# A hybrid encoder trunk: mixer halved by token parity and spread over its input projection, and the keys' mean by a block matrix with a re-ordered end of the attention

## Chip, cores and metric

One core of one Trainium2 chip. The metric is device microseconds of one execution; the kernel before has a median of 1862.9 us over 3 runs (1862.3 to 1864.59).

## What is computed

Two sequences of 256 tokens pass two layers with the same weights, model width 1024. Each layer is half an FFN, a mixer, half an FFN. The mixer of layer 0 pools four channel groups over windows of 2, 4, 8 and 16 tokens beside a long convolution by FFT; the mixer of layer 1 is a neighbourhood attention of 16 heads of 64 with normalised queries and keys. Cut to these two:

```python
def pool_hyena_mixer(xn, ...):
    p = xn @ w_in                                  # 1024 -> 512 + 3 * 512
    a = pool_mixer(p[..., :POOL_WIDTH], pool_w, pool_scale)   # (win_sum / cnt - u) @ w_grp * scale
    hb = short_conv(p[..., POOL_WIDTH:], short_w, short_b)    # three taps
    x0, x1, v = hb[..., :512], hb[..., 512:1024], hb[..., 1024:]
    k_f = hyena_filter_fft(L, ...)                 # rfft of (MLP of t * decays), 2 L points
    yh = fftconv(v * x1, k_f, h_bias) * x0         # irfft(rfft(u, 2 L) * k_f)[:L] + u * bias
    return concatenate([a, yh]) @ w_out

def na_mixer(xn, w_qkv, gq, gk, rpb, w_o):
    q, k, v = split(xn @ w_qkv)
    q, k = rmsnorm(q, gq), rmsnorm(k, gk)          # mean of squares over the 64 features of a head
    out = softmax(where(col_mask, q @ k.T * scale + bias, -inf)) @ v
    return out @ w_o
```

## The kernel before

All 512 tokens lie as columns and the features on partitions, 8 chunks of 128 for the width. The program runs through phases one after the other: the first FFN, w_in, w_out, two FFNs, qkv, w_o, the last FFN. Each engine has a block of its own (sync, scalar, vector, tensor, gpsimd) whose instructions are written out in the order in which it runs them; semaphores join the engines, so the order by hand decides everything. A **unit** of a projection is 128 output features by 512 tokens in one PSUM bank: 8 steps of k, each three fp32r matmuls (`three`, L1241: high by high, low by high, high by low parts, L1242, L1245, L1246). Its weights arrive by DMA, ACT rounds them to the high part (`split_high`, L480) and VectorE subtracts that for the low part (`split_low`, L489), about two units ahead. A unit can have **hooks**: other work of TensorE put in front of step k. Matmuls outside the units are plain fp32 and show as two records each.

w_in has 16 units, (i, j) for i in 0 to 3 and j in 0 to 3. For each i VectorE takes the banks out times the norm factor (`scaled`, L883), ACT and VectorE make the three-tap convolutions (L548, L901, L904), VectorE the product v * x1, TensorE turns that product (L1367), and POOL makes the window sums (L1633 to L1644). The filter's decays (ACT, L794, L797) and its products and sums (L1196 to L1207) lie in between. Only after all 16 units come the Fourier steps, as matmuls with cosine and sine matrices: filter spectra (L1541, 8 matmuls), token spectra (L1553, 16), pool matmuls (L1560, 4), inverse (L1569, 32); VectorE multiplies spectra (L1224) and POOL sums them. Then w_out starts.

qkv runs 8 pairs of heads of three units (query, key, value); the attention of pair p - 1 is worked in hooks of pair p (`attention`, L1370 on TensorE, L1084 on VectorE, L679 on ACT). At a pair's end the means of squares of queries and keys are made by two-column matmuls (`squares_mean`, L1415), ACT takes the square root (L730), VectorE the reciprocal of 128x16 (L1139), copies the keys' part wide (L1141), TensorE turns it (`key_factor`, L1423), VectorE scales the key (L1145) and takes the value (L883, tile vt). From the third pair on, the first unit of a pair is in the bank of the value unit before it, and `bank_read` makes it wait until vt has been taken. `three` and the wait in `unit`:

```python
if ph.name == "qkv":
    return (0, 1, 2 if isinstance(i, int) and i == 0 else 0)[j]
...
if ks[0] == 0 and (ph.name == "qkv" or isinstance(i, int) and i == 0 and j == 0):
    pe.wait_ge(*bank_read(ph, i, j))
```

After pair 7, w_o's first two units (7 of their 8 steps) hold the last pair's scores, turns (L1393) and values (L1402) in hooks; the rest of w_o follows.

## Time and profile before

| what | value |
|---|---|
| median of 3 runs | 1862.9 us (1862.3 to 1864.59) |
| the profiled execution's own time | 1859.85 us |
| its span, first to last instruction | 1858.1 us |
| TensorE busy | 1848.1 us, 99% |
| VectorE busy | 1310.8 us, 71% |
| ACT busy | 819.9 us, 44% |
| POOL busy | 292.3 us, 16% |
| granted TensorE clock | 1.00 |
| share of the chain that ended last | TensorE 98%, VectorE 1% |

The profile is of one execution. Busy times are sums over the span; the chain is followed back from the last instruction, so a share of 98% says that TensorE's own instructions, one behind the other, fill the time. Time starts in each row are us from the start of the span.

### The profile page before, as it was taken

How to read it: one execution, taken by the hardware profiler on the slowest of the kernel's cores; microseconds unless marked ns; L12 is line 12 of the kernel's file. 1: busy time of each engine (PE TensorE's matmuls, PEld its weight loads, DVE VectorE, ACT ScalarE, POOL GpSimd, SP SyncE). 2: the span in 40 equal slices, each digit the busy share in tenths (PEclk: the TensorE clock that was granted, in tenths of full speed). 3: DMA queues.
4: the chain of work that ended last, by engine and by line, in shares of the span. 5: the costliest groups of instructions: out<-in, count | busy, mean ns of one | idle time of the engine just before them, and what ended most of it. 6: DMA issues, size and time to landing. Idle time of an engine off the chain costs nothing.

```text
span 1858.1 us, 26529 instructions
## 1 busy us (share of the span) xinstructions
PE 1848.1 (99%) x10116; PEld 1581.6 (85%) x10116; DVE 1310.8 (71%) x2086; ACT 819.9 (44%) x1344; POOL 292.3 (16%) x247
## 2 busy tenths in 40 slices
PE   9999999999999999999999999999999999999999
PEld 7898988977688988989889898898777788989889
DVE  7686865975466867768767686686776666868666
ACT  5343443643244433435534343465655543433333
POOL 0210401203301203102021130111111002104011
PEclk9999999999999999999999999999999999999999
DMA  5244236632032222348323223662222232332356
GB/s 186 75 142 119 91 114 173 166 127 91 23 114 102 102 97 86 114 123 229 102 74 131 91 91 114 181 156 86 70 80 79 74 114 74 113 110 90 111 159 162
DMA packets 79737, 210.70 MB, mean 113 GB/s; under 512 B 15144, under 2 KB 28105, under 8 KB 79626
## 3 DMA queue, kind: packets, MB, share of 16 engines
q1 hardware_dynamic: 56800, 182.48, 28.6%
q0 software_dynamic: 9216, 16.78, 5.3%
q10 hardware_dynamic: 13610, 9.93, 1.9%
q8 instruction: 73, 1.20, 0.3%
q14 instruction: 38, 0.31, 0.1%
HBM read 190.29 MB, written 3.93 MB: 105 GB/s over the span
## 4 chain that ended last, share of the span: by engine, by line
PE 98%; DVE 1%; ACT 0%; DMA 0%; issue 0%; SPq 0%; ACTq 0%; DVEq 0%
PE bank L1290 25%; PE bank L1292 25%; PE bank L1291 25%; PE bank L1242 6%; PE bank L1245 5%; PE bank L1246 5%; PE bank L1402 1%; PE bank L1569 1%; PE bank L1553 1%; PE bank L1415 1%; PE bank L1393 1%; PE bank L1423 0%; PE bank L1541 0%; PE bank L1382 0%; DMA x<-in_x_tokens 0%; PE bank L1345 0%
## 5 line engine op out<-in xcount | busy, mean ns | idle before, releaser
L1290 PE MATMUL bank<-xh,whr 128*128 128x512 f32 x1408 | 551.5, 392 | 2.3 <-DVE wlr L466 1.0
L1291 PE MATMUL bank<-xl,whr 128*128 128x512 f32 x1408 | 549.1, 390 | 0.0
L1292 PE MATMUL bank<-xh,wlr 128*128 128x512 f32 x1408 | 549.0, 390 | 0.0
L457 ACT ACTIVATE whr<-rest 128x512 fp32r<-128x512 f32 (+1 forms) x445 | 273.2, 616 | 455.4 <-PE bank L1292 445.5
L466 DVE TENSOR_TENSOR wlr<-rest,whr 128x512 fp32r<-128x512 f32 (+1 forms) x445 | 323.3, 730 | 124.5 <-ACT whr L457 121.7
L1290 PE MATMUL bank<-hsh,whr 128*128 128x256 f32 x1232 | 349.1, 283 | 0.4 <-issue 0.3
L1291 PE MATMUL bank<-hsl,whr 128*128 128x256 f32 x1232 | 348.6, 283 | 0.0
L1292 PE MATMUL bank<-hsh,wlr 128*128 128x256 f32 x1232 | 348.6, 283 | 0.0
L1290 PEld LDWEIGHTS bank<-xh,whr 128*128 128x128 f32 x1408 | 265.1, 188 | 60.0 <-issue 2.1
L1292 PEld LDWEIGHTS bank<-xh,wlr 128*128 128x128 f32 x1408 | 265.0, 188 | 55.7
L1291 PEld LDWEIGHTS bank<-xl,whr 128*128 128x128 f32 x1408 | 265.1, 188 | 55.4 <-issue 1.0
L457 ACT ACTIVATE whr<-raw_area 128x512 fp32r<-128x512 f32 (+1 forms) x243 | 147.6, 608 | 238.7 <-PE bank L1292 233.8
L1290 PEld LDWEIGHTS bank<-hsh,whr 128*128 128x128 f32 x1232 | 236.3, 192 | 1.4 <-DVE wlr L466 0.5
L1291 PEld LDWEIGHTS bank<-hsl,whr 128*128 128x128 f32 x1232 | 236.4, 192 | 0.5
L1292 PEld LDWEIGHTS bank<-hsh,wlr 128*128 128x128 f32 x1232 | 236.4, 192 | 0.0
L466 DVE TENSOR_TENSOR wlr<-raw_area,whr 128x512 fp32r<-128x512 f32 (+1 forms) x243 | 173.1, 715 | 61.8 <-ACT whr L457 60.4
L976 DVE SCALAR_TENSOR_TENSOR x<-bank,x 128x256 f32<-128x256 f32 (+1 forms) x288 | 146.3, 508 | 5.3 <-PE bank L1292 3.7
L928 DVE TENSOR_TENSOR ga<-bank,rbc 128x512 f32<-128x512 f32 x88 | 60.8, 691 | 77.6 <-PE bank L1292 77.5
L1242 PE MATMUL bank<-xh,whr 128*128 128x512 f32 x256 | 103.5, 404 | 0.0
L1588 POOL TENSOR_TENSOR raw_area<-raw_area 128x384 f32<-128x384 f32 (+1 forms) x14 | 17.3, 1235 | 527.1 <-DMA raw_area<-in_ffn_w_down 527.1
L1245 PE MATMUL bank<-xl,whr 128*128 128x512 f32 x256 | 100.0, 391 | 0.0
L1246 PE MATMUL bank<-xh,wlr 128*128 128x512 f32 x256 | 99.8, 390 | 0.0
(188 smaller groups left out, 2114.6 us busy)
## 6 DMA issues: line engine op xcount, KB each, us to landing
rest<-in_ffn_w_up SPq DMA_DIRECT2D x62, 512.0 KB, 4.7
rest<-in_ffn_w_gate SPq DMA_DIRECT2D x61, 512.0 KB, 3.8
rest<-in_ffn_w_down SPq DMA_DIRECT2D x54, 512.0 KB, 4.6
raw_area<-in_ffn_w_gate SPq DMA_DIRECT2D x26, 512.0 KB, 3.7
raw_area<-in_ffn_w_up SPq DMA_DIRECT2D x26, 512.0 KB, 4.7
raw_area<-in_ffn_w_down SPq DMA_DIRECT2D x26, 512.0 KB, 4.6
raw_area<-in_w_qkv SPq DMA_DIRECT2D x24, 512.0 KB, 3.4
rest<-rest POOLq DMA_DIRECT2D x38, 256.0 KB, 4.6
```

Source lines behind the costliest of these rows:

```text
L457: act.activation(whr[:, at:at + st.kb, :].rearrange("p k c -> p (k c)"), weights(st, buf)[:, 0, :], ACT.Copy).then_inc(high, 1)
L466: dve.tensor_tensor(wlr[:, at:at + st.kb, :].rearrange("p k c -> p (k c)"), weights(st, buf)[:, 0, :], whr[:, at:at + st.kb, :].bitcast(F3 ...
L928: dve.tensor_tensor(ga[st.tiles % 2][:, :], bank[st.bank][:, :], rbc[:, :], ALU.mult).then_inc(evac, 1)
L976: dve.scalar_tensor_tensor(out=out, in0=src, scalar=0.5 * sign, in1=out, op0=ALU.mult, op1=ALU.add)\
L1242: pe.matmul(out, wh[w][:, k, :], hi[:, at, :], start=start, stop=False)
L1245: pe.matmul(out, wh[w][:, k, :], lo[:, at, :], start=False, stop=False)
L1246: return pe.matmul(out, wl[w][:, k, :], hi[:, at, :], start=False, stop=stop)
L1290: pe.matmul(out, whr[:, at, :], hi, start=start, stop=False, skip_group_check=onto)
L1291: pe.matmul(out, whr[:, at, :], lo, start=False, stop=False, skip_group_check=onto)
L1292: return pe.matmul(out, wlr[:, at, :], hi, start=False, stop=stop, skip_group_check=onto)
L1393: last = pe.transpose(bank[2 if h % 2 else 6][:, k * SEQ + t * P:k * SEQ + (t + 1) * P], sc[:, h, t, k * P:(k + 1) * P], ident)
L1402: last = pe.matmul(bank[7][a_ * HD:(a_ + 1) * HD, s * SEQ:(s + 1) * SEQ], vs[:, 2 * s + k, a_ * HD:(a_ + 1) * HD], pt[:, h % 2, k, :], sta ...
```

## The change

Three edits are made at once.

- **The mixer.** Tokens are parted into even and odd ones, so that the cosine and sine matrices have 128 frequencies by 128 tokens of a parity: half as many or half as wide matmuls (filter spectra 4 of 512 columns, L1562; token spectra 16 of 256, L1586; inverse 32 of 128, L1599). Sums and differences of the halves give the full spectra; VectorE makes them and the products, and POOL only the window sums. The work is done for each i by itself, and TensorE's part stands in hooks of w_in's units and of w_out's first two, whose steps go in the order 3, 2, 1, 4, 5, 0, 6, 7. Units of one i are now v, x1, pool, x0; the largest pool window comes first. ACT's and VectorE's orders for w_in are written anew.
- **The keys.** Their mean of squares is one plain 128x512 matmul with a block matrix of 1/64 (`key_mean`), so that it stands for each key on all partitions of its head. ACT's square root and VectorE's reciprocal run over 128x512 (L808, L1367), and the key is scaled from SBUF (L1369). The wide copy and `key_factor` are gone. The queries keep their two-column matmuls (`query_mean`).
- **The end of the attention.** w_o's third unit is begun early in bank 3 and shares the last pair's hooks with the first two; its split comes first on ACT and VectorE, and the banks of the first two units are taken after the fourth unit's split.

```diff
-                return w_in[bass.ds((3 - j) * KH + i, 1)]
+                return w_in[bass.ds((3 * KH + i, 2 * KH + i, KH - 1 - i, KH + i)[j], 1)]
...
+                if attends and not projects:
+                    split_high(act, by["w_o"], 0, 2)
...
-                    act.wait_ge(ms_mm, p + 1)
-                    act.activation(rqk[:, :, :, :], bank[3][:, 0:4 * TT].rearrange("p (a t h) -> p a t h", a=2, t=TT),
-                                   ACT.Sqrt, bias=cst[:, C_EPS:C_EPS + 1]).then_inc(ms_std, 1)
+                    act.wait_ge(k_mean, p + 1)
+                    act.activation(rk[:, :], bank[3][:, :], ACT.Sqrt, bias=cst[:, C_EPS:C_EPS + 1]).then_inc(k_std, 1)
                     if attends:
                         act.wait_ge(s_mm, 4 * p)
                     act.activation(qh[:, :], qt[:, :], ACT.Copy).then_inc(qh_done, 1)
+                    act.wait_ge(q_mean, p + 1)
+                    act.activation(rq[:, :, :], bank[3][:, 0:2 * TT].rearrange("p (t h) -> p t h", t=TT), ACT.Sqrt,
+                                   bias=cst[:, C_EPS:C_EPS + 1]).then_inc(q_std, 1)
...
+                def products(i):
+                    dve.wait_ge(wide_done, 2 * (i + 1))
+                    dve.wait_ge(kf_done, 2)
+                    if i:
+                        dve.wait_ge(spec_done, 2 * i)
+                    for n, out in enumerate((t1, t2)):
+                        dve.tensor_tensor(out[:, :, :, :], wide[:, :, :, :],
+                                          kfb[:, :, n, i * P:(i + 1) * P].unsqueeze(2).to_broadcast([P, 2, 2 * NSEQ, P]),
+                                          ALU.mult).then_inc(prod_done, 1)
+                def product_sums(i):
+                    dve.wait_ge(prod_done, 2 * (i + 1))
+                    for n, op in enumerate((ALU.subtract, ALU.add)):
+                        own_, other = slice(NSEQ * n, NSEQ * (n + 1)), slice(NSEQ * (1 - n), NSEQ * (2 - n))
+                        dve.tensor_tensor(t1[:, :, own_, :], t1[:, :, own_, :], t2[:, :, other, :], op).then_inc(sum_done, 1)
...
+                split(0, 0)
+                norm_factor(NORM_OF["w_in"])
+                split(0, 1)
+                take(0, 0)
+                take(0, 1)
+                sums_cleared(NORM_OF["w_in"])
+                taps(0, 0)
+                taps(0, 1)
+                product(0)
+                split(0, 2)
+                to_pool(0)
+                filter_in_time()
+                split(0, 3)
+                take(0, 3)
+                filter_sums()
+                taps(0, 3)
+                for i in range(1, KH):
+                    if i > 1:
+                        gate_with(i - 2)
+                    split(i, 0)
+                    take(i, 0)
+                    if i > 1:
+                        products(i - 1)
+                    taps(i, 0)
+                    if i == 1:
+                        filter_in_frequency()
+                    take(i, 1)
+                    split(i, 1)
+                    taps(i, 1)
+                    product(i)
+                    if i == 1:
+                        frequencies(0)
+                    else:
+                        product_sums(i - 1)
+                        conv_low(i - 2)
+                    split(i, 2)
+                    to_pool(i)
+                    if i == 1:
+                        products(0)
+                        pool_low(0)
+                        product_sums(0)
+                        spectra(0)
+                    else:
+                        spectra(i - 1)
+                        pool_low(i - 1)
+                    if i == KH - 1:
+                        frequencies(i)
+                        products(i)
+                    split(i, 3)
+                    take(i, 3)
+                    if i < KH - 1:
+                        taps(i, 3)
+                        frequencies(i)
+                i = KH - 1
+                product_sums(i)
+                spectra(i)
+                gate_with(i - 1)
+                taps(i, 3)
+                pool_low(i)
+                conv_low(i - 1)
+                gate_with(i)
+                conv_low(i)
...
-                    dve.wait_ge(ms_std, p + 1)
-                    dve.reciprocal(rqk[:, :, :, :], rqk[:, :, :, :]).then_inc(rqk_done, 1)
-                    dve.wait_ge(rqk_done, p + 1)
-                    dve.tensor_copy(kwide[:, :, :].rearrange("p t (h c) -> p t h c", h=2),
-                                    rqk[:, 1, :, :].unsqueeze(3).to_broadcast([P, TT, 2, HD])).then_inc(kw_done, 1)
-                    dve.wait_ge(kb_mm, p + 1)
-
-                    dve.scalar_tensor_tensor(out=kt[:, :], in0=kt[:, :], scalar=gqk[:, 0:1], in1=bank[3][:, :],
+                    dve.wait_ge(k_std, p + 1)
+                    dve.reciprocal(rk[:, :], rk[:, :]).then_inc(rk_done, 1)
+                    dve.wait_ge(rk_done, p + 1)
+                    dve.scalar_tensor_tensor(out=kt[:, :], in0=kt[:, :], scalar=gqk[:, 0:1], in1=rk[:, :],
                                              op0=ALU.mult, op1=ALU.mult).then_inc(kn_done, 1)
+                    dve.wait_ge(q_std, p + 1)
+                    dve.reciprocal(rq[:, :, :], rq[:, :, :]).then_inc(rq_done, 1)
                     if attends:
                         dve.wait_ge(v_mm, p)
                     scaled(ph, p, 2, vt[:, :], unit_bank(ph, p, 2))
...
+                def filter_frequencies():
+                    pe.wait_ge(filt_done, 8)
+                    for n in range(4):
+                        q, cs = n // 2, n % 2
+                        pe.matmul(bank[4 + n][:, :], dft[:, cs, q, :], (hdif if cs else hsum)[:, q, :], start=True,
+                                  stop=True).then_inc(kf_mm, 1)
...
+                def inverse(c):
+                    pe.wait_ge(spec_done, 2 * (c + 1))
+                    pe.wait_ge(ut_done, min(c + 2, KH))
+                    if c:
+                        pe.wait_ge(gated, c)
+                    for s in range(NSEQ):
+                        for q in range(2):
+                            at = (2 * s + q) * P
+                            for cs in range(2):
+                                last = pe.matmul(bank[6][:, at:at + P], spec[c % 2][:, q, NSEQ * cs + s, :],
+                                                 idft[:, q, cs, :], start=cs == 0, stop=cs == 1)
+                    last.then_inc(inv_mm, 1)
...
+                norm = NORM_OF["w_in"]
+                unit(ph, 0, 0, waits=[(xl_done, chunk_base(norm) + k + 1) for k in range(KD)])
+                unit(ph, 0, 1, hooks={1: lambda: norm_mean(norm)})
+                unit(ph, 0, 2, hooks={4: filters})
+                unit(ph, 0, 3)
+                for i in range(1, KH):
+                    if i == 1:
+                        unit(ph, 1, 0)
+                        unit(ph, 1, 1, hooks={4: filter_frequencies})
+                        unit(ph, 1, 2, hooks={2: lambda: turn_u(0), 5: lambda: frequencies(0), 6: lambda: pool_mm(0)})
+                    else:
+                        unit(ph, i, 0, hooks={4: lambda: inverse(i - 2)})
+                        unit(ph, i, 1, hooks={5: lambda: pool_mm(i - 1)})
+                        unit(ph, i, 2)
+                    last = {7: lambda: inverse(KH - 2)} if i == KH - 1 else {}
+                    unit(ph, i, 3, hooks={1: lambda: turn_u(i), 4 + (i < KH - 1): lambda: frequencies(i), **last})
+                ph = by["w_out"]
+                order = [3, 2, 1, 4, 5, 0, 6, 7]
+                parts = [(pool_al, KH - k) if k < KH else (conv_al, k - KH + 1) for k in range(KD)]
+                unit(ph, 0, 0, waits=parts, ks=order[:5], order=order, hooks={2: lambda: pool_mm(KH - 1)})
+                unit(ph, 0, 1, ks=order[:5], order=order, hooks={1: lambda: inverse(KH - 1)})
+                for j in range(2):
+                    unit(ph, 0, j, waits=parts, ks=order[5:], order=order)
...
-                def squares_mean():
-                    pe.wait_ge(sqq_done, p + 1)
+                def key_mean():
                     pe.wait_ge(sqk_done, p + 1)
+                    pe.wait_ge(heads_done, 4)
                     if attends:
                         pe.wait_ge(vs_done, p)
-                    for a_, sq in enumerate((sqq, sqk)):
-                        for t in range(TT):
-                            at = a_ * 2 * TT + 2 * t
-                            last = pe.matmul(bank[3][:, at:at + 2], sq[:, t * P:(t + 1) * P], cst[:, C_HEAD:C_HEAD + 2],
-                                             start=True, stop=True)
-                    last.then_inc(ms_mm, 1)
-
-                def key_factor(pair=p):
-
-                    pe.wait_ge(kw_done, pair + 1)
+                    pe.matmul(bank[3][:, :], heads[:, :], sqk[:, :], start=True, stop=True).then_inc(k_mean, 1)
...
                 def turn_values():
                     pe.wait_ge(evac, by["qkv"].group(p - 1, 2) + 1 + EVAC_CREDIT)
-                    pe.wait_ge(kn_done, p)
+                    pe.wait_ge(q_std, p)
                     for t in range(TT):
...
-                    unit(ph, 0, 0, waits=parts, ks=ks, hooks={1: leftovers, 2: first_scores, 6: lambda: scores(1)})
+                    unit(ph, 0, 0, waits=parts, ks=ks, hooks={1: leftovers, 2: first_scores})
                     pe.wait_ge(evac, ph.group0 - 1 + EVAC_CREDIT)
-                    unit(ph, 0, 1, ks=ks, hooks={0: lambda: (turn(0), turn(1)), 3: first_values,
-                                                 4: lambda: (turn(2), turn(3)), 5: lambda: second_values(p - 1)})
+                    unit(ph, 0, 1, ks=ks, hooks={1: lambda: scores(1), 4: lambda: (turn(0), turn(1))})
+                    pe.wait_ge(vs_done, PAIRS)
+                    unit(ph, 0, 2, ks=range(6), hooks={0: first_values, 2: lambda: (turn(2), turn(3)),
+                                                               4: lambda: second_values(p - 1)})
                     for j in range(2):
                         unit(ph, 0, j, waits=parts, ks=[KD - 1])
+                    unit(ph, 0, 2, waits=parts, ks=range(6, KD))
...
-                if isinstance(p, int):
-                    unit(ph, p, 0, hooks={1: lambda: key_factor(0), 4: leftovers})
-                else:
-                    unit(ph, p, 0, hooks={2: leftovers})
+                unit(ph, p, 0, hooks={2: leftovers})
                 first_scores()
                 unit(ph, p, 1)
-                unit(ph, p, 2, hooks={1: second_scores, 4: first_values, 5: squares_mean, 7: key_factor})
+                unit(ph, p, 2, hooks={1: second_scores, 4: first_values, 5: key_mean, 7: query_mean})
```

VectorE at the end of a pair, before (rsum: softmax sums, rqk: both root means, kt and vt: key and value, ms_std: ACT's root, kb_mm: the turned factor):

```order
L1107 TENSOR_SCALAR sc<-sc,rsum 128x256 [waits rs_done]
L1107 TENSOR_SCALAR sc<-sc,rsum 128x256
L1139 RECIPROCAL rqk<-rqk 128x16 [waits ms_std]
L1141 COPY kwide<-rqk 128x512 [waits rqk_done]
L1145 SCALAR_TENSOR_TENSOR kt<-kt,small,bank 128x512 [waits kb_mm]
L879 REGISTER_ALU [waits v_mm]
L883 TENSOR_TENSOR vt<-bank,rbc 128x512 [waits unit_done]
```

and with the change (rk, rq: root means of keys and queries apart):

```order
L1330 TENSOR_SCALAR sc<-sc,rsum 128x256 [waits rs_done]
L1330 TENSOR_SCALAR sc<-sc,rsum 128x256
L1367 RECIPROCAL rk<-rk 128x512 [waits k_std]
L1369 SCALAR_TENSOR_TENSOR kt<-kt,small,rk 128x512 [waits rk_done]
L1372 RECIPROCAL rq<-rq 128x8 [waits q_std]
L947 REGISTER_ALU [waits v_mm]
L951 TENSOR_TENSOR vt<-bank,rbc 128x512 [waits unit_done]
```

The reciprocal has grown from 128x16 to 128x512 and stands ahead of kt and vt; the copy and the wait for kb_mm are gone.

VectorE behind w_in's last units, before (spec, ga, ua: parts of the products of spectra, kf: filter spectra):

```order
L489 TENSOR_TENSOR wlr<-raw_area,whr 128x1024 [waits high]
L883 TENSOR_TENSOR ppad<-bank,rbc 128x2x256 [waits unit_done]
L489 TENSOR_TENSOR wlr<-raw_area,whr 128x1024 [waits high]
L1224 TENSOR_TENSOR spec<-bank,kf 128x512 [waits u_mm,tap_done,kf_done]
L1224 TENSOR_TENSOR spec<-bank,kf 128x512
L1224 TENSOR_TENSOR ga<-bank,kf 128x512 [waits u_mm]
L1224 TENSOR_TENSOR ua<-bank,kf 128x512
```

and with the change, around unit (1,2) (wide: a spectrum's halves joined, kfb: filter spectra, t: products, ppad: the pool input that POOL waits for):

```order
L501 TENSOR_TENSOR wlr<-raw_area,whr 128x1024 [waits high]
L951 TENSOR_TENSOR ppad<-bank,rbc 128x2x256 [waits unit_done]
L1041 TENSOR_TENSOR t<-wide,kfb 128x1024 [waits kf_done,wide_done]
L1041 TENSOR_TENSOR t<-wide,kfb 128x1024
L1075 SCALAR_TENSOR_TENSOR al<-bank,small,ah 128x512 [waits pool_ah]
L1050 TENSOR_TENSOR t<-t 128x2x256 [waits prod_done]
L1050 TENSOR_TENSOR t<-t 128x2x256
L1058 TENSOR_TENSOR spec<-t 128x512 [waits sum_done]
L1058 TENSOR_TENSOR spec<-t 128x512
L501 TENSOR_TENSOR wlr<-raw_area,whr 128x1024 [waits high]
```

The products now stand between the splits of two units, right behind ppad, and what TensorE's first inverse needs is the spec at the end.

TensorE in unit (2,0) with the change, where no Fourier step stood before:

```order
L1428 MATMUL bank<-xh,whr 128x512
L1431 MATMUL bank<-xl,whr 128x512
L1432 MATMUL bank<-xh,wlr 128x512
L1599 MATMUL bank<-idft,spec 128x128 [waits ut_done,spec_done]
L1599 MATMUL bank<-idft,spec 128x128 x7
L1428 MATMUL bank<-xh,whr 128x512
```

The inverse's eight matmuls stand ahead of step 4 and wait for spec; the unit's own steps are behind them.

## Rows read from the trace of the kernel before

**Rows 1.** The page's fourth part: the chain that ended last, shares of the span by engine.
```profile
PE 98%; DVE 1%; ACT 0%; DMA 0%; issue 0%; SPq 0%; ACTq 0%; DVEq 0%
```

**Rows 2.** The chain in order of time (start, duration, engine and line), w_in to w_out.
```profile
365.76 0.45 PE bank L1242
...
460.17 6.87 PE bank L1541 x16
467.04 13.73 PE bank L1553 x32
...
484.20 13.81 PE bank L1569 x64
```

**Rows 3.** TensorE in order of time in w_out (start, duration, line, operation, out<-in, count).
```profile
499.24 0.39 PE L1242 MATMUL bank<-ah,whr 128*128 128x512 f32 x1
...
540.04 0.39 PE L1242 MATMUL bank<-ah,whr 128*128 128x512 f32 x1
```

**Rows 4.** VectorE in order of time, the norm ahead of w_in and w_in.
```profile
374.61 3.35 DVE L870 RECIPROCAL rbc<-rbc 128x512 f32<-128x512 f32 x1 [0.70 <-ACT rbc L537]
...
395.35 2.48 DVE L1196 SCALAR_TENSOR_TENSOR filt<-decay,bank 128x512 f32<-128x512 f32 x4 [1.65 <-ACT decay L797]
...
398.51 1.23 DVE L1202 TENSOR_TENSOR hsum<-filt 128x1024 f32<-128x1024 f32 x1
...
401.52 1.21 DVE L489 TENSOR_TENSOR wlr<-raw_area,whr 128x1024 fp32r<-128x1024 f32 x1
...
461.78 2.16 DVE L489 TENSOR_TENSOR wlr<-raw_area,whr 128x1024 fp32r<-128x1024 f32 x1 [1.32 <-ACT whr L480]
```

**Rows 5.** POOL in order of time, window sums of w_in.
```profile
393.86 1.08 POOL L1633 TENSOR_TENSOR win<-ppad 128x542 f32<-128x542 f32 x1 [26.12 <-DVE ppad L883]
395.02 1.30 POOL L1640 TENSOR_TENSOR win<-win,icnt 128x512 f32<-128x512 f32 x1
...
461.77 4.45 POOL L1633 TENSOR_TENSOR win<-win 128x538 f32<-128x538 f32 x3
```

**Rows 6.** ACT in order of time, the norm ahead of w_in and the decays.
```profile
373.89 0.69 ACT L537 ACTIVATE rbc<-bank,small 128x512 f32<-128x512 f32 x1
...
394.09 2.19 ACT L797 ACTIVATE decay<-absd,small 128x1024 f32<-128x1024 f32 x2
```

**Rows 7.** Busy time by windows: PE, PEld, DVE, ACT, POOL, clock, DMA share, GB/s.
```profile
378.00:380.00 2.00, 2.00 (x10) 1.65 (x10) 0.97 (x1) 0.93 (x1) 0.00 (x0) 1.00 0.15 61
```

**Rows 8.** TensorE in order of time, the end of a pair of the attention.
```profile
1389.23 0.95 PE L1415 MATMUL bank<-small,sqq 128*128 128x2 f32 x8
...
1394.94 0.50 PE L1242 MATMUL bank<-xh,whr 128*128 128x512 f32 x1
```

**Rows 9.** VectorE in order of time, the same end.
```profile
1388.45 1.94 DVE L1107 TENSOR_SCALAR sc<-sc,rsum 128x256 f32<-128x256 f32 x2
...
1390.50 0.62 DVE L1107 TENSOR_SCALAR sc<-sc,rsum 128x256 f32<-128x256 f32 x2
...
1393.51 0.75 DVE L1145 SCALAR_TENSOR_TENSOR kt<-kt,small,bank 128x512 f32<-128x512 f32 x1 [1.38 <-PE bank L1423]
1394.20 0.69 DVE L883 TENSOR_TENSOR vt<-bank,rbc 128x512 f32<-128x512 f32 x1
```

**Rows 10.** ACT and POOL in order of time, the same end.
```profile
1389.49 1.28 ACT L730 ACT_TABLE_LOAD   x1
...
1388.43 1.55 POOL L1658 TENSOR_TENSOR bmask<-braw,small 128x768 f32<-128x768 f32 x1 [18.38 <-DVE nmax L1098]
1391.98 1.28 POOL L1665 TENSOR_TENSOR ql<-qt,qh 128x512 fp32r<-128x512 f32 x1 [2.00 <-ACT qh L734]
```

**Rows 11.** TensorE in order of time, the end of the attention.
```profile
1447.57 0.47 PE L1242 MATMUL bank<-oh,whr 128*128 128x512 f32 x1
...
1462.26 1.47 PE L1402 MATMUL bank<-pt,vs 128*64 128x256 f32 x8 [1.97 <-ACT pt L707]
...
1481.09 0.39 PE L1242 MATMUL bank<-oh,whr 128*128 128x512 f32 x1
```

More of the change, by code:

```diff
@@ L334, in unit_bank @@
                 return (0, 1, 2 if isinstance(i, int) and i == 0 else 0)[j]
+            if ph.name == "w_o" and isinstance(i, int) and i == 0:
+                return (0, 1, 3, 2)[j]
             return j
@@ new lines, in to_pool, with filter_in_time @@
+                def to_pool(i):
+                    scaled(ph, i, 2, ppad[:, KH - 1 - i, :, PAD:PAD + SEQ], 2, "p (s t) -> p s t")
+                def filter_in_time():
+                    for t in range(2):
+                        for half in range(2):
+                            n = 2 * t + half
+                            dve.wait_ge(filt_mm, n + 1)
+                            dve.wait_ge(dec_done, 2 + t)
+                            dve.scalar_tensor_tensor(out=filt[:, t, half, :], in0=decay[:, t, half, :], scalar=0.05,
+                                                     in1=bank[4 + n][:, :], op0=ALU.add, op1=ALU.mult)\
+                               .then_inc(filt_done, 1)
@@ L1258, in bank_read, with unit @@
                 else:
-                    look = 1 if at_start else 3
+                    look = 1 if at_start else 2 if ph.name == "w_o" and j == 2 else 3
                 return evac, ph.group(i, j) - look + EVAC_CREDIT
-            def unit(ph, i, j, waits=None, hooks={}, ks=None):
+            def unit(ph, i, j, waits=None, hooks={}, ks=None, order=None):
                 w = split_place(ph, i, j)[0]
@@ L1280, in unit @@
                         pe.wait_ge(*waits[k])
-                    last = three(bank[b][:, :], w, k, b, hi, lo, k, start=k == 0, stop=k == ph.kt - 1,
-                                 between=after if k == ph.kt - 1 else None)
-                if ks[-1] == ph.kt - 1:
+                    last = three(bank[b][:, :], w, k, b, hi, lo, k, start=k == order[0], stop=k == order[-1],
+                                 between=after if k == order[-1] else None)
+                if ks[-1] == order[-1]:
                     last.then_inc(unit_done, 1)
@@ L1496, in _ @@
                     continue
-                def first(ph=ph, name=name):
-                    if name in NORM_OF:
-                        norm = NORM_OF[name]
-                        unit(ph, 0, 0, waits=[(xl_done, chunk_base(norm) + k + 1) for k in range(KD)])
-                        unit(ph, 0, 1, hooks={1: lambda: norm_mean(norm)})
-                        rest = range(2, ph.per)
-                    else:
-                        if name == "w_o":
-                            attention(PAIRS, False, True, False)
-                            rest = range(2, ph.per)
-                        else:
-                            unit(ph, 0, 0, waits=[(al_done, k + 1) for k in range(KD)])
-                            rest = range(1, ph.per)
-                    for j in rest:
-                        unit(ph, 0, j)
-                    if name == "w_in":
-                        turn_u(0)
-                        pe.wait_ge(mix_in, 16 * 7)
-                        for n in range(4):
-                            t, half = n // 2, n % 2
-                            if n == 3:
-                                pe.wait_ge(ut_done, 1)
-                            pe.matmul(bank[4 + n][:, :], h3[:, t * P:(t + 1) * P], fwo[:, half * HW:(half + 1) * HW],
-                                      start=True, stop=True).then_inc(filt_mm, 1)
@@ L1524, in body @@
-                def body(i, last, ph=ph, name=name):
+                if name == "w_in":
+                    w_in_run(ph)
+                    continue
+                if name == "w_o":
+                    attention(PAIRS, False, True, False)
+                for j in range(3 if name == "w_o" else 2, ph.per):
+                    unit(ph, 0, j)
+                with pe.Fori(1, ph.iters) as i:
                     for j in range(ph.per):
                         unit(ph, i, j)
-                    if name == "w_in":
-                        turn_u(i)
```

454 lines of the change are left out of this document (255 added, 199 removed).

## Prediction

> **What bounds the kernel now.** I read the chain that ended last first: TensorE holds 98% of it, VectorE 1%, all else next to nothing [rows 1]. The matmuls themselves set the time; an edit pays only by taking work off TensorE, and costs only where it makes TensorE wait. Next, the chain in order of time [rows 2]: w_in begins at 365.76, and after its 16 units three stretches of plain fp32 matmuls stand alone on TensorE: filter spectra 6.87 us (L1541), token spectra 13.73 (L1553), inverse 13.81 (L1569). Then the rate of the units: from 499.24 to 540.04 [rows 3] lie 60 steps of k, three 512-column matmuls each, 0.68 a step and 5.44 a unit, without a gap. Last, the end of an attention pair [rows 8 to 10] and of the attention [rows 11], the two other places that are edited.
>
> **The mixer.** Its multiplications on TensorE [rows 2]: the filter spectra go from 8 to 4 matmuls of 512 columns, 6.87 / 2 = 3.43; the token spectra keep 16 matmuls but of 256 columns instead of 512, 13.73 / 2 = 6.87; the inverse keeps its 32 matmuls (64 records) but of 128 columns instead of 256, 13.81 / 2 = 6.9. No row has short fp32 matmuls in this number, so I take 7.1, a little over half (the two-column ones of the attention, 8 records in 0.95 [rows 8], say that a record goes down to some 0.12 at least). Turns, filter matmuls and pool matmuls stay. Sum: 3.44 + 6.86 + 6.7 = **17.0 us off TensorE**.
>
> These pieces now sit inside units, so each one whose input is late stops TensorE. I followed the new order of VectorE (quoted ahead) with durations of before: a split 1.21, a 128x1024 product or sum 1.23 [rows 4], a bank's take 0.69 [rows 9], the rest by the same rate.
> 1. filter_frequencies stands in unit (1,1) before step 4: 365.76 + five units + 0.86 + 3.43 (norm and filter matmuls) + 2.72 = about 400.0. The constants have landed by 378, from when on DMA's share is 0.15 [rows 7]; decays follow them (1.04, a table load of 1.28 and 2.19 [rows 6]), to 382.5; ACT's split(0,1) is behind them, done at 383.6. VectorE then has, in order: the split, two takes, the memset, four taps, two products, a split, to_pool, four filter products, a split, a take, memset, sum, difference and bias, 17 us with semaphore gaps: 401.5, and 402.7 if POOL's window sums hold one up. Wait: **2.0**.
> 2. inverse(0) is in unit (2,0) before step 4, 10.3 us after unit (1,2) ends (unit, turn 0.44, spectra 1.72, half a unit). VectorE's to_pool ends 2.95 after that point, then two products, pool_low, two product sums, two spectra: 5.7, done at 8.7, no wait. But the same to_pool starts POOL's five window steps, and rows show such steps and VectorE's two-input instructions taking turns: a split took 2.16 instead of 1.21 when it began beside a window sum at 461.77, and those three POOL sums took 4.45 where one alone takes 1.08 [rows 4, 5]. Taking turns, some five POOL steps of about 1.1 come between: 14.0 instead of 8.7. Wait: **3.7**.
> 3. turn_u(2) behind the same queue 1.0; inverse(3) in w_out, at the end of product sums, spectra and taps, 2.0; w_out's third split 0.4; the rest 0.6 as an allowance. Sum **4.0**.
>
> Mixer: -17.0 + 2.0 + 3.7 + 4.0 = **-7.3**. If nothing takes turns, waits 2 and parts of 3 go: about -13.6.
>
> A rule is to be weighed against rows here. In the mixer, filter products (one input in PSUM, one in SBUF) ran 2.48 for four beside POOL's 1.30 at 395.02, neither stretched [rows 4, 5], while the two-input split was. The Trainium skill ("SBUF — State Buffer", Who interferes with whom) says the same in general: a VectorE instruction with two SBUF inputs contends with a GpSimd one that reads SBUF, with the lock held for a whole instruction; one with at most one SBUF input, outside the 2-port modes, doesn't. By it the mixer's sum is as above, and the attention's long reciprocal shuts nobody out.
>
> **The keys of a pair.** Let S be the start of the mean squares, 1389.23, where now unit (p+1,0) follows at 1394.94, S + 5.71 [rows 8]. What releases it is VectorE's take of vt, 1394.20 + 0.69 [rows 9], since the unit writes the bank that vt is read from. The new chain: key_mean 0.86 (13.73 / 16), hidden by ACT's table load to S + 1.54 [rows 10]; Sqrt of 128x512, 0.69 as in the norm [rows 6], to S + 2.27; VectorE's **RECIPROCAL of 128x512, 3.35** as in the norm [rows 4], to S + 5.62, where before it took 128x16; kt 0.75 to 6.40; rq about 0.15; vt to 7.24; TensorE at S + 7.29. Removed are the copy of kwide, key_factor on TensorE and VectorE's wait for it. TensorE itself is ready earlier: means 0.86 + 0.84, three steps and turns 0.9, S + 4.65, so its work is no cover and it waits 2.6. Per pair 7.29 - 5.71 = 1.58, seven times: **+11.1**; the first pair, whose unit has another bank, waits only for vt before its turn: +0.4. ACT's kh and the next splits are 1.4 later but need to be ready only within unit (p+1,0): hidden.
>
> Bounds: if ACT's Sqrt and POOL are as above, nothing makes this smaller except a unit that isn't held by vt (rival 2); if POOL's ql (1.28, ready S + 2.9 [rows 10]) can't run beside the reciprocal, kt waits for it too (rival 3).
>
> **The end of the attention.** w_o starts at 1447.57, waits 1.97 at 1462.26 for the probabilities' copy, and unit (1,0) starts at 1481.09, 33.5 later [rows 11]. With the third unit as a filler that wait goes. But split(0,2) now stands ahead of the first maxima on VectorE (1.45 later), unit (0,3) finds its split 1.05 late since its buffer is free only after unit (0,1), and unit (1,0) finds its split behind two residuals, some 1.6 with what is left of the first wait: unit (1,0) at 32.65. **-0.85**.
>
> **Sum.** -7.3 + 11.1 + 0.4 - 0.85 = +3.35 on the profiled execution's 1859.85: 1863.2. That execution lies 3.05 under the median of 1862.9, so the forecast for the median is **1866**. About 0.2% (3.7 us) is what a measurement can tell from no change; this lies just inside.
>
> **Rivals.**
> 1. *POOL and VectorE collide less.* The window sums may begin in gaps that VectorE has for ACT's splits anyway; for it, the filter products beside POOL; against it, the stretched split. Mixer -12 to -15, so 1858 to 1862. On the fast side. Chance 0.22.
> 2. *The reciprocal doesn't gate the next unit.* If unit (p+1,0) isn't held by vt, TensorE goes on at S + 4.65, saving 1.06 a pair: 7 x 1.06 + 0.85 = 8.3 won in the attention, 15.6 in all: 1847. For it, TensorE waits nowhere for vt now in the list of waits; against it, 1394.20 + 0.69 = 1394.89 and the start at 1394.94. Chance 0.10.
> 3. *The long reciprocal shuts POOL out* (slower). Place: between rk's reciprocal and kt; price: ql's 1.28 a pair, seven times, 9.0; point: whether ql starts before or after the reciprocal ends. For it: two one-input TENSOR_SCALARs took 1.94 beside POOL's mask at 1388.43, and 0.62 without [rows 9, 10]. Against it: filter products with one input in SBUF weren't held [rows 4, 5]. 1875. By the skill's rule, the reciprocal has one SBUF input and isn't held, so this would be 0; TENSOR_SCALAR is among those that it lists with 2-port modes. Chance 0.10.
> 4. *Short matmuls aren't half as long* (slower). If 128-column inverse records took as long as 256-column ones, the saving of 6.7 goes: 1873. Against it: the chain's two-column means are down to 0.12 a record, little over half of the inverse's 13.81 / 64 = 0.216. Chance 0.08.
>
> **How the numbers follow.** The forecast has 0.50: spread of some 5 us about 1866 from stalls that I estimated (0.05 faster, 0.25 same, 0.20 slower). Rival 1 splits 0.11 faster, 0.11 same; rival 2 is faster; 3 and 4 slower. Faster 0.26, same 0.36, slower 0.38. The range goes from 1853 (rival 1 with shorter waits at the end) to 1875 (rival 3); outside are rival 2 and the far tails.
>
> **What would show it.** Mixer: TensorE's busy time between w_in's and w_out's start down by 17, its waits at L1562, L1577, L1586 and L1599 near 9 in sum; right if inverse(0) waits over 2 us on VectorE's spectra. Attention: a TensorE wait of 2.6 in each of seven pairs, ended by vt, period 27.8 instead of 26.25, the reciprocal 3.35. If the waits for vt are absent, rival 2; if ql starts after the reciprocal, rival 3. TensorE's granted clock should stay at 1.00, its level of 2.4 GHz, as after the 1.97 wait at 1462.26, behind which matmuls went on at 0.227. Wrong altogether if the period hasn't changed or if w_out starts over 15 us earlier.

## The result, and the profile after

The changed kernel takes **1868.14 us** (median of 14 runs, 1863.3 to 1871.88) against 1862.1 (14 runs, 1858.99 to 1865.02): ratio 1.0033, 95% interval 1.0025 to 1.0042, slower by 0.33%. 1866 was forecast, in a range of 1853 to 1875; "slower" and "same" had 0.38 and 0.36. The forecast stood on a median of 1862.9 before and a change of +3.35; the change measured is +6.0. The profiled execution (1863.3, span 1861.5) is the fastest of the 14, which will matter below. One run of the kernel before beside the experiments, 3075 us at a mean clock of 0.555, is left out throughout.

The page of the changed kernel, busy times and chain [rows 1]:

```profile
PE 1827.2 (98%) x9996; PEld 1560.5 (84%) x9996; DVE 1351.9 (73%) x2112; ACT 825.2 (44%) x1354; POOL 288.8 (16%) x239
...
PE 85%; DVE 6%; DMA 4%; issue 3%; ACT 2%; SPq 0%; POOL 0%; ACTq 0%; DVEq 0%; POOLq 0%
```

TensorE is busy 20.9 us less than before (1848.1), yet the span is 3.4 us longer, and VectorE and DMA have come into the chain. Where TensorE stood still, by what it waited for (total, times, longest):

```profile
PE bank L1428 <- DVE vt L951: 12.3, 6, 2.1
PE bank L1428 <- DVE wlr L501: 2.6, 3, 1.1
...
PE bank L1477 <- DVE x L1199: 2.3, 3, 1.4
PE bank L1599 <- DVE spec L1058: 2.2, 1, 2.2
PE bank L1428 <- issue: 2.1, 1, 2.1
PE bank L1562 <- DVE hsum L1017: 1.6, 1, 1.6
...
PE bank L1691 <- DVE vt L951: 1.3, 1, 1.3
...
PE bank L1599 <- DVE x L1065: 0.6, 1, 0.6
```

The waits for vt and the one by "issue" (the last pair's, in front of w_o; vt was done 0.1 us before it ended) are the ends of the attention pairs, 15.7 us together; those for spec and hsum and for x at L1599 are the mixer's hooks, 4.5 us; wlr is the low part of split weights, in w_out and w_o. The stretches between the first matmuls of the phases, read from TensorE in order of time:

| stretch | before | after | difference |
|---|---|---|---|
| start to w_in | 365.74 | 366.57 | +0.8 |
| w_in to the next FFN (mixer) | 175.66 | 164.71 | **-10.95** |
| two FFNs | 703.54 | 704.83 | +1.3 |
| qkv to w_o (pairs) | 202.63 | 214.95 | **+12.3** |
| w_o to the last FFN | 55.28 | 55.47 | +0.2 |

The FFNs were not edited. Waits for x there (here 2.3 us in three) differ in length and place from profile to profile, also in kernels where only another phase was changed. They make part of the differences: in the two FFNs TensorE stood still 0.9 us after the change and 0.3 before it, so the rest of the +1.3 is not explained.

**The mixer**, TensorE in order of time: the hooks that waited [rows 2 had these pieces as stretches of their own], and where w_out starts.

```profile
403.20 1.12 PE L1562 MATMUL bank<-hsum,dft 128*128 128x512 f32 x2 [1.65 <-DVE hsum L1017]
...
430.79 2.05 PE L1599 MATMUL bank<-idft,spec 128*128 128x128 f32 x16 [2.21 <-DVE spec L1058]
...
483.42 0.39 PE L1428 MATMUL bank<-ah,whr 128*128 128x512 f32 x1
...
489.89 2.02 PE L1599 MATMUL bank<-idft,spec 128*128 128x128 f32 x16 [0.64 <-DVE x L1065]
...
498.51 0.50 PE L1428 MATMUL bank<-ah,whr 128*128 128x512 f32 x1 [0.43 <-DVE wlr L501]
```

Before, w_out started here:

```profile
497.67 0.58 PE L1242 MATMUL bank<-ah,whr 128*128 128x512 f32 x1
```

VectorE, and POOL, in front of the wait for spec:

```profile
421.14 3.24 DVE L1041 TENSOR_TENSOR t<-wide,kfb 128x1024 f32<-128x1024 f32 x2
...
424.98 2.39 DVE L1050 TENSOR_TENSOR t<-t 128x512 f32<-128x512 f32 x2
...
427.40 3.34 DVE L1058 TENSOR_TENSOR spec<-t 128x512 f32<-128x512 f32 x2
```

```profile
421.37 1.94 POOL L1830 TENSOR_TENSOR win<-ppad 128x542 f32<-128x542 f32 x1 [18.77 <-DVE ppad L951]
423.39 3.43 POOL L1830 TENSOR_TENSOR win<-win 128x538 f32<-128x538 f32 x2
```

The same instructions for the next i ran while POOL stood still, but for the start of a step beside the spectra:

```profile
440.08 2.35 DVE L1041 TENSOR_TENSOR t<-wide,kfb 128x1024 f32<-128x1024 f32 x2
...
447.77 1.29 DVE L1050 TENSOR_TENSOR t<-t 128x512 f32<-128x512 f32 x2
...
451.31 1.28 DVE L1058 TENSOR_TENSOR spec<-t 128x512 f32<-128x512 f32 x2
```

Two 128x1024 products took 3.24 instead of 2.35; the two sums and two spectra behind them took 5.73 in all instead of 2.57; POOL's first three steps alongside took 1.94 and 1.72 each (3.43 for two) instead of 1.08 to 1.30 [rows 5]. They take turns, as the forecast had it, but from the end of ppad's take to spec it is 9.5 us, not 11.

**A pair's end**, VectorE [rows 9], then POOL [rows 10] and TensorE [rows 8], with the start of the key's mean (L1677) and the next units:

```profile
1361.41 3.35 DVE L1367 RECIPROCAL rk<-rk 128x512 f32<-128x512 f32 x1 [0.40 <-ACT rk L808]
1364.80 0.75 DVE L1369 SCALAR_TENSOR_TENSOR kt<-kt,small,rk 128x512 f32<-128x512 f32 x1
1365.47 0.20 DVE L1372 RECIPROCAL rq<-rq 128x8 f32<-128x8 f32 x1
1365.58 0.64 DVE L951 TENSOR_TENSOR vt<-bank,rbc 128x512 f32<-128x512 f32 x1
```

```profile
1361.98 1.28 POOL L1853 TENSOR_TENSOR ql<-qt,qh 128x512 fp32r<-128x512 f32 x1 [2.10 <-ACT qh L811]
```

```profile
1310.88 0.50 PE L1428 MATMUL bank<-xh,whr 128*128 128x512 f32 x1 [2.05 <-DVE vt L951]
...
1338.56 0.50 PE L1428 MATMUL bank<-xh,whr 128*128 128x512 f32 x1 [2.05 <-DVE vt L951]
...
1359.14 1.02 PE L1677 MATMUL bank<-sqk,small 128*128 128x512 f32 x2
...
1366.28 0.50 PE L1428 MATMUL bank<-xh,whr 128*128 128x512 f32 x1 [2.06 <-DVE vt L951]
...
1395.55 0.50 PE L1428 MATMUL bank<-xh,whr 128*128 128x512 f32 x1 [2.06 <-DVE vt L951]
```

The reciprocal takes 3.35, vt ends at 1366.22, and the unit starts at 1366.28. The starts lie 27.7 apart, except the last two: 29.27. Before, a pair took 26.25, from the mean of squares of one pair, here, to that of the next at 1389.23 [rows 8]:

```profile
1362.97 0.95 PE L1415 MATMUL bank<-small,sqq 128*128 128x2 f32 x8
```

What made 29.27 is in the windows (the seventh number, not counting those in brackets, is the granted clock):

```profile
1366.00:1368.00 2.00, 1.72 (x7) 1.39 (x8) 1.02 (x2) 2.00 (x4) 1.29 (x1) 0.93 0.00 0
1368.00:1370.00 2.00, 2.00 (x11) 1.24 (x11) 0.67 (x1) 0.14 (x1) 0.00 (x0) 0.50 0.08 8
1370.00:1372.00 2.00, 2.00 (x9) 1.13 (x6) 0.00 (x0) 1.09 (x2) 0.00 (x0) 0.71 0.74 254
1372.00:1374.00 2.00, 2.00 (x11) 1.62 (x9) 0.69 (x1) 0.00 (x0) 0.00 (x0) 1.00 0.38 104
```

TensorE waited 2.06 us until 1366.28, and from about 1368 to 1371 its clock was granted at 0.50, its level of 1.2 GHz; 1.6 us were lost. Below, such a stretch is called a fall. After the other vt waits of this execution the clock stayed at 1.00.

### The profile page after: what moved, and what is told of

Its sections match the earlier page's. It is cut to its first block, busy times and chain, and to the rows that moved or that the text cites. A ratio compares the mean times of both kernels' runs of the same rounds, so it can differ in the third digit from the quotient of the medians.

```text
span 1861.5 us, 26232 instructions
## 1 busy us (share of the span) xinstructions
PE 1827.2 (98%) x9996; PEld 1560.5 (84%) x9996; DVE 1351.9 (73%) x2112; ACT 825.2 (44%) x1354; POOL 288.8 (16%) x239
## 4 chain that ended last, share of the span: by engine, by line
PE 85%; DVE 6%; DMA 4%; issue 3%; ACT 2%; SPq 0%; POOL 0%; ACTq 0%; DVEq 0%; POOLq 0%
PE bank L1477 24%; PE bank L1478 23%; PE bank L1479 23%; PE bank L1428 4%; PE bank L1431 4%; PE bank L1432 4%; DMA rest<-rest 2%; DVE rk L1367 1%; PE bank L1667 1%; DVE wlr L501 1%; DVE t L1041 0%; PE bank L1658 0%; DVE sc L1316 0%; ACT whr L492 0%; DMA rest<-in_ffn_w_down 0%
## 5 line engine op out<-in xcount | busy, mean ns | idle before, releaser
L1428 PE MATMUL bank<-xh,whr 128*128 128x512 f32 x256 | 106.4, 416 | 12.3 <-DVE vt L951 12.3
```

The source lines that it names most:

```text
L1428: pe.matmul(out, wh[w][:, k, :], hi[:, at, :], start=start, stop=False)
```

## Experiments

**Each edit alone.** The kernel before with one of the three edits, as the diff ahead of the prediction has it: mixer_alone with `w_in_run` on the three engines, POOL's order and the constants; keys_alone with `key_mean`, `query_mean` and the reciprocal of 128x512; end_alone with w_o's third unit as a filler.

> The mixer's edit alone, keys and end of the attention as before. By the two traces, w_in's start to the first matmul of the next FFN went from 175.7 to 164.7 us, so the mixer alone should be some 11 us faster than the kernel before, near 1851 (ratio about 0.994), with a granted clock of 1.00 in all runs, as its longest wait is about 2.2 us and the units around it are full. Rival, that the loss of the whole change sits in the mixer (the FFNs around it starting later): this kernel would be no faster than before.

> The keys' edit alone, mixer and end of the attention as before. If vt's take behind the long reciprocal is what costs, w_o starts 12 us later than before and the time is 1874 or more (ratio 1.006 to 1.010), with seven waits of 2.05 us on vt. If these waits also let the clock down now and then, as between 1368 and 1371 in the profile of the change, the runs differ among themselves by up to 10 us, with mean clocks from 0.994 to 1.000, and the median is nearer to 1877. Rival, that the slow pairs come from the mixer's new order of weights and DMA: this kernel would be within 0.3% of before.

> The re-ordered end of the attention alone. By the traces unit (1,0) of w_o starts 33.5 us after unit (0,0) in both kernels, so nothing: within 0.1% of before. My prediction's -0.85 us would be 0.9995. The wait of 1.97 us for the probabilities' copy goes, and two waits of about 1.1 us on split weights take its place.

| kernel | median | ratio, 95% interval | mean clock of its runs |
|---|---|---|---|
| mixer_alone | 1853.61 | 0.9946 (0.9929 to 0.9963) | 0.997 to 1.000 |
| keys_alone | 1876.16 | 1.0070 (1.0053 to 1.0086) | 0.996 to 0.998 |
| end_alone | 1862.10 | 0.9993 (0.9983 to 1.0003) | 0.999 to 1.000 |

The mixer's stretch is 164.68 us, as in the whole change; its median is 9.3 us lower, and the 11 of the trace lie within the interval. Its clock was expected at 1.00 in all runs and was not: the profiled one fell at a wait of 2.85 us in an FFN (ended at 353.87), which no edit touches. keys_alone loses 13 us; its pairs take 216.44 from qkv to w_o, and it has the same waits (1.28, six of 2.05 to 2.06, 2.10). Its runs lie within 4 us of each other, not up to 10. The end is not told from zero. The three ratios multiply to 1.0009, below the 1.0033 of the whole; their intervals are too wide to make more of it. keys_alone's clock in the windows of the first fall:

```profile
1294.00:1296.00 2.00, 2.00 (x10) 1.58 (x9) 1.34 (x1) 1.60 (x3) 1.05 (x1) 0.77 0.00 0
1296.00:1298.00 2.00, 2.00 (x10) 0.80 (x9) 0.14 (x1) 0.00 (x0) 0.00 (x0) 0.50 0.26 66
1298.00:1300.00 2.00, 2.00 (x9) 1.49 (x8) 0.34 (x1) 1.09 (x2) 0.00 (x0) 0.88 0.53 205
```

It falls after the wait that ended at 1293.73, again after those that ended at 1406.14 and 1477.89 (1.99, for pt in w_o), and not after the other five vt waits that stopped a first matmul.

**Does the wait let the clock down?** One run, 1904.65 us:

```diff
+                    dve.reciprocal(sqk[:, :], rk[:, :])
                     dve.reciprocal(rk[:, :], rk[:, :]).then_inc(rk_done, 1)
```

> The change with the keys' reciprocal computed twice (once into a scratch tile). If VectorE's chain from the square root to vt is all that gates the next unit, each of the seven waits grows by 3.35, from 2.05 to 5.40, and the span by 7 x 3.35 and the first pair's 3.35: 1861.5 + 26.8 = 1888. If a wait lets the clock down, now more of the seven are followed by a stretch at half clock, each some 1.6 us more: up to 1898 for all seven. Rival, that another chain ends close behind: less than 3.35 a pair is added.

The span was 1902.8, above the 1888 to 1898 that were expected. TensorE's waits, the first pair's, a middle pair's and w_o's, and the windows around the second:

```profile
1262.20 1.11 PE L1692 MATMUL bank<-small,vt 128*128 128x128 f32 x4 [4.49 <-DVE vt L951]
...
1359.34 0.79 PE L1429 MATMUL bank<-xh,whr 128*128 128x512 f32 x1 [5.27 <-DVE vt L951]
...
1490.72 0.77 PE L1429 MATMUL bank<-oh,whr 128*128 128x512 f32 x1 [5.32 <-issue]
```

```profile
1288.00:1292.00 4.00, 0.00 (x0) 0.00 (x0) 3.96 (x4) 0.10 (x1) 0.00 (x0) 0.84 0.00 0
1292.00:1296.00 4.00, 3.41 (x10) 2.69 (x10) 2.00 (x2) 2.45 (x4) 1.29 (x1) 0.50 0.00 0
1296.00:1300.00 4.00, 4.00 (x19) 2.55 (x18) 0.69 (x1) 1.09 (x2) 0.00 (x0) 0.81 0.42 131
```

The waits grew by 3.19 to 3.22 each, nearly the whole 3.35, so VectorE's chain with the reciprocal is what gates. A second chain that starts from the same reciprocal would be late with it, so this run can't exclude one. And now a stretch of low clock comes with **every one** of the eight waits, here from within the wait on. qkv to w_o is 253.64, 38.7 more than in the change: 25.7 are the longer waits, so 13.0 are left for six more stretches of low clock, 2.2 each and not 1.6, which is where the forecast of this run fell short. After a wait of 2.05 the clock fell at times, with one of 5.27 each time.

**Taking the gate away.** VectorE takes vt between two halves of the reciprocal:

```diff
-                    dve.reciprocal(rk[:, :], rk[:, :]).then_inc(rk_done, 1)
+                    dve.reciprocal(rk[:, 0:SEQ], rk[:, 0:SEQ])
+                    if attends:
+                        dve.wait_ge(v_mm, p)
+                    scaled(ph, p, 2, vt[:, :], unit_bank(ph, p, 2))
+                    dve.reciprocal(rk[:, SEQ:TOK], rk[:, SEQ:TOK]).then_inc(rk_done, 1)
...
-                    if attends:
-                        dve.wait_ge(v_mm, p)
-                    scaled(ph, p, 2, vt[:, :], unit_bank(ph, p, 2))
+                    dve.wait_ge(rq_done, p + 1)
```

> The whole change, but the keys' reciprocal cut in two halves of 256 tokens and the take of vt put between them. If it is vt behind the reciprocal that gates the next unit, the seven waits of 2.05 us go, a pair takes about 25.2 us instead of 27.7 (less than the 26.25 of before, since key_factor and the small squares are off TensorE), and the time is 1862 - 11 - 7 = 1844 (ratio about 0.990), all runs at a clock of 1.00 and close together. Rival, that TensorE is held by kt or by the next splits instead: the wait only moves to the scores or to unit (p+1,1), and the time stays over 1860.

1873.16, ratio 1.0052 (1.0036 to 1.0069), clock 0.994 to 0.996: a miss, by the rival's way. TensorE no longer waits for vt, but in the middle of the next unit:

```profile
1284.80 1.56 PE L1669 MATMUL bank<-pt,vs 128*64 128x256 f32 x8 [2.42 <-ACT pt L784]
...
1313.36 1.65 PE L1669 MATMUL bank<-pt,vs 128*64 128x256 f32 x8 [2.45 <-ACT pt L784]
```

The key is finished later, and on ACT the copy kh, which waits for the key, stands in front of the weight split and the probabilities' copies pt that the values need. So the next step moved kh behind them:

```diff
-                    act.wait_ge(kn_done, p + 1)
-                    act.activation(kh[:, :], kt[:, :], ACT.Copy).then_inc(kh_done, 1)
                     split_high(act, *ahead(ph, p, 2, last))
                 if attends:
                     probs_t(2)
                     probs_t(3)
+                if projects:
+                    act.wait_ge(kn_done, p + 1)
+                    act.activation(kh[:, :], kt[:, :], ACT.Copy).then_inc(kh_done, 1)
```

> As vt_between, and on ACT the copy kh, which waits for the key, put behind the weight split and the copies of the turned probabilities (pt), for which TensorE waited 2.45 us a pair in vt_between. If kh in front of pt was what held TensorE, no wait over 0.5 us is left in the seven pairs, a pair takes 27.7 - 2.05 = 25.65 us, 0.6 less than before the change, the clock stays at 1.00 in all runs, and the time is 1862 - 10 - 7 x 0.6, about 1848 (ratio 0.992). Rival, that the key itself comes too late for the next scores: the wait moves there and the time stays over 1860.

1848.05, ratio 0.9928 (0.9914 to 0.9941). qkv to w_o is 196.79 us, 5.8 less than before and 18.2 less than in the change, and no wait in the seven pairs is left. The clock of its runs was 0.998 to 1.000, not 1.00 in all; of the four waits over 1.5 us that its profile has left, one, at the first inverse, was followed by a fall. One wait that is new stands in w_o's first unit, for the key's low part:

```profile
1439.00 0.39 PE L1650 MATMUL bank<-kh,qh 64*128 64x256 f32 x2 [1.62 <-POOL kl L1858]
```

**POOL out of VectorE's way.** The four steps ahead of the subtraction are left out of POOL's window sums for i = 1 (one run, 1862.54 us, read by its trace):

```diff
-                for n in range(g + 1):
+                if i != 1:
+                    for n in range(g + 1):
...
```

> The change, with POOL's window sums for i = 1 left out (its four steps before the subtraction; so pooled values of that group aren't the reference's). If POOL's steps taking turns with VectorE's products make spec late, VectorE's six instructions there go from 9.5 us back to about 5.8 to 7 and TensorE's wait of 2.21 us at the first inverse is gone. Rival, that VectorE is late through its own queue: the wait stays at 2 us or more.

VectorE in the same place, and POOL's one remaining step:

```profile
422.32 3.42 DVE L1041 TENSOR_TENSOR t<-wide,kfb 128x1024 f32<-128x1024 f32 x2
425.66 0.74 DVE L1075 SCALAR_TENSOR_TENSOR al<-bank,small,ah 128x512 fp32r<-128x512 f32 x1
426.32 1.28 DVE L1050 TENSOR_TENSOR t<-t 128x512 f32<-128x512 f32 x2
427.64 1.29 DVE L1058 TENSOR_TENSOR spec<-t 128x512 f32<-128x512 f32 x2
```

```profile
422.53 2.13 POOL L1843 TENSOR_TENSOR ppad<-win,ppad 128x512 f32<-128x512 f32 x1 [18.77 <-issue]
```

The wait for spec is gone, and the mixer's stretch is 162.10, 2.6 less. Beside the one step the products still took 3.42; the sums and spectra, beside nothing, 2.6 instead of 5.73. So POOL's steps beside VectorE's were what made spec late.

**Hooks later.** Two kernels on top of vt_between_act move w_in's hooks.

```diff
-                        unit(ph, i, 0, hooks={4: lambda: inverse(i - 2)})
+                        unit(ph, i, 0, hooks={7 if i == 2 else 4: lambda: inverse(i - 2)})
```

> As vt_between_act, and the first inverse in front of step 7 of unit (2,0) instead of step 4, so that 2.04 us of matmuls lie where TensorE waited 2.21 for spec. If nothing else hangs on the inverse's place, 2 us less than vt_between_act: about 1846 (ratio 0.991). If the work behind it (turn, spectra, w_out's first units) waits for it, the wait comes again later and the time is the same.

1847.47, 0.9925 (0.9911 to 0.9938), not told from vt_between_act. The wait for spec is gone, but the next turn now waits 1.26 and a weight split 0.30; and the filter hook's wait of 1.94 was followed by a clock fall (0.66 in 404 to 408). The mixer's stretch was 166.72, against 166.20.

```diff
-                        unit(ph, 1, 1, hooks={4: filter_frequencies})
+                        unit(ph, 1, 1, hooks={7: filter_frequencies})
...
-                        unit(ph, i, 0, hooks={4: lambda: inverse(i - 2)})
-                        unit(ph, i, 1, hooks={5: lambda: pool_mm(i - 1)})
+                        unit(ph, i, 0, hooks={} if i == 2 else {4: lambda: inverse(i - 2)})
+                        unit(ph, i, 1, hooks={**({0: lambda: inverse(0)} if i == 2 else {}), 5: lambda: pool_mm(i - 1)})
...
```

> As vt_between_act, with the hooks of w_in that waited put later: filter_frequencies in front of step 7 of unit (1,1) instead of 4, turn and spectra of i = 0 two steps and one step later, the first inverse in front of unit (2,1), turn and spectra of i = 2 later by two and one steps, the last inverse one step later. The waits there were 1.61, 2.21, 0.62 and 0.43 in vt_between_act, and a clock fall after the second cost 1.1. If VectorE's work keeps its times, some 4 us go, from 166.2 between w_in and the FFN to about 162, and the time is about 1844 (ratio 0.990). Rival, as in inverse_later, where 2.2 went and 1.6 came back at the next turn: the waits only move, and the time stays at 1847.

**1846.07** (4 runs, 1844.15 to 1848.96), ratio **0.9912** (0.9895 to 0.9928): 17 us faster than the kernel before, and the lowest median of all. The mixer's stretch is 163.01; its waits are 0.71, 0.64, 1.30 and 0.44, none followed by a fall. About 3 of the 4 us came there, about half of them the fall that vt_between_act had behind its first inverse (its stretch of 166.20 was 164.71 in the change, with the same waits and no fall). The wait of 1.62 for the key's low part in w_o was followed by a fall here (0.50 from 1436 to 1438) and was not in vt_between_act. Against vt_between_act alone its lead of 2 us isn't shown by the intervals.

## Why the prediction was right, point by point

The number came out near for reasons that are half right: two terms were off in opposite directions and one was left out. The mechanisms hold (work off TensorE in the mixer, waits at its hooks, vt behind the long reciprocal); that the sizes cancel is luck.

- **Work off TensorE, -17.0.** The mixer's stretch went down by 10.95 with 4.93 us of waits at hooks and w_out (1.65, 2.21, 0.64, 0.43). That leaves 15.9 for the work, 1.1 under the forecast; TensorE's busy time in the stretch says the same, 159.8 against 175.6. I take the rest to be the starts of the hooks, not measured apart. Rival 4 (short records not halved) fell: 16 inverse records took 2.05, 0.128 each, against 0.216. One sign of being wrong came out at its edge: w_out starting over 15 us earlier. It starts 14.3 us earlier (483.42 against 497.67), and 15.1 if counted from w_in's start. The sign was badly chosen, as w_out now holds hooks and their waits: it takes 47.9 us to the next FFN, where it took 43.7.
- **The mixer's waits, 9.7: mis-sized.** They are 4.9. The filter's hook was 1.65 (2.0 forecast). The inverse's was 2.21 (3.7): turns are taken, as no_window_sums shows, but VectorE needed 9.5 us for its six instructions and not 11. The wait at turn_u(2) (1.0) did not come, the last inverse's was 0.64 (2.0). So the mixer gained 10.95 and not 7.3; this lies nearly at rival 1's -12, with the turns taken and the waits shorter.
- **The keys, +1.58 a pair.** Shown: wait for vt 2.05 (2.6), reciprocal 3.35, period 27.7 (27.8 in the forecast), 1.45 a pair. From the start of the key's mean, S = 1359.14, the unit starts at S + 7.14 (7.29); the wait was over-sized since TensorE's own work lasts to S + 5.08, not 4.65. By reciprocal_twice this chain gates, and vt_between and vt_between_act show what stood close behind, ACT's kh. Rival 2 fell. Rival 3 fell: ql ran at 1361.98 inside the reciprocal of 1361.41 to 1364.76, at its usual 1.28. The Trainium skill ("SBUF — State Buffer", Who interferes with whom) was right on both sides here: one SBUF input, no contention (3.35 as in the norm, 1.28 as before the change); two, turns, as the products and sums beside POOL's steps.
- **The clock, left out: the step that failed.** I wrote that the granted clock "should stay at 1.00", from one wait of 1.97 behind which it had. That one wait was no evidence for seven more: after waits of 2.05 it fell at times, for some 1.6 us of loss each. The profiled execution had one fall of 3.4 us (mean clock 0.999). The 14 runs have mean clocks of 0.994 to 0.999, 0.9966 on average: 2 x 0.0034 x 1866 is some 12.5 us at half clock a run, or 3.7 falls of that length. The kernel before is not free of falls: its profiled execution has none but at its very end, and its 32 runs beside the experiments have 0.9993 on average, some 0.8 falls a run. So a typical run after the change has some 2.7 falls more than its profiled execution, one before it 0.8 more; the 1.9 between them are an estimated 3.0 us at 1.6 each. The medians lie 4.8 and 2.25 us above the two profiled executions, 2.6 apart; with the 3.4 between the spans this is the 6.0. Where the falls of the runs without a trace stand, and so how many of them belong to vt's waits, is not on record.
- **The end, -0.85.** Measured +0.2 in the trace, and end_alone 0.9993 (0.9983 to 1.0003). Its mechanism was as told, 1.97 for pt replaced by 1.11 and 1.08 for split weights:

```profile
1477.76 0.50 PE L1428 MATMUL bank<-oh,whr 128*128 128x512 f32 x1 [1.11 <-DVE wlr L501]
...
1484.60 0.50 PE L1428 MATMUL bank<-oh,whr 128*128 128x512 f32 x1 [1.08 <-DVE wlr L501]
```

  The step that was mis-sized: from w_o's start to unit (0,3) without the wait lie 25.6 us of TensorE's work (1476.65 - 1451.06), where I had counted 24.6 (32.65 less a unit of 5.44 and the waits of 1.05 and 1.6).

The sum for one execution was +3.35 and the spans differ by 3.4; that is a mixer 3.7 better and an attention, end and FFNs 3.7 worse than told, the FFNs' part of some 2 us with nothing in the forecast. The agreement to 0.1 us is luck. One reading was off without effect: ql starts at S + 2.75 by its row, not 2.9.

## What to carry to other kernels

Where an instruction grows, ask which buffer release stands behind it in the same queue and who waits for that; put the release ahead, and then look at what the later result holds up in each queue that waits for it (here the move on VectorE alone gave 0.5% slower, and with the move on ACT it was 0.7% faster; the one on ACT alone was not run). A wait of TensorE can cost more than its length, as the clock may fall with it (1.6 us behind a wait of 2.06), so judge a kernel with many such waits by the clocks of several runs and not by one profile. Work moved into hooks should stand where the other engine's queue has its input ready, with that engine's neighbours (POOL's steps) counted in.

## What was not expected of the hardware

TensorE's granted clock after waits. In the eleven traces, past the opening, none of the 58 waits of 0.35 to 1.55 us had a fall within 3 us of its end, 14 of the 52 of 1.6 to 3.1 did (3 of 17 under 2.0, 6 of 27 from 2.0 to 2.2, 5 of 8 from 2.4 on), and all 8 of 4.5 to 5.3, these in one run. One of 2.21 in vt_between_act made the inverse's 16 records take 3.17 instead of 2.05, and the same wait in the change did nothing:

```profile
431.13 3.17 PE L1602 MATMUL bank<-idft,spec 128*128 128x128 f32 x16 [2.21 <-DVE spec L1059]
```

What decides for those in the middle was not tried and stays open.
